# Block 0 of each later expert: its hidden rows turned by VectorE in 16 squares instead of by TensorE

## What is computed

```python
def swiglu(h, w_gate_up, w_down):
    g, u = jnp.split(h @ w_gate_up, 2, axis=-1)
    return (jax.nn.silu(g) * u) @ w_down

def moe_ffn(h, router, w_gate_up, w_down):
    ...
    for e in range(N_EXPERTS):
        out = out + combine[:, e:e + 1].astype(t.dtype) * swiglu(t, w_gate_up[e], w_down[e])
```

## Time and profile before

| what | value |
|---|---|
| median of 3 runs | 1422.05 us |
| the profiled execution's own time | 1421.34 us |
| its span | 1419.6 us |
| TensorE busy | 1412.5 us (99%) |
| VectorE busy | 1233.3 us (87%) |
| ScalarE busy | 963.5 us (68%) |
| share of TensorE in the chain that ended last | 96% |

### The profile page before, as it was taken

The page is one execution under the profiler, slowest core; times in us unless marked ns, Lnnn a source line. Parts: engine busy times, 40 slices in busy tenths (PEclk is TensorE's granted clock), DMA queues, the critical chain, the costliest instruction groups (busy, mean ns, idle before and its releaser), DMA issues.

```text
span 1419.6 us, 19929 instructions
## 1 busy us (share of the span) xinstructions
PE 1412.5 (99%) x6741; PEld 1187.1 (84%) x6741; DVE 1233.3 (87%) x1201; ACT 963.5 (68%) x839; POOL 100.2 (7%) x146
## 2 busy tenths in 40 slices
PE   9999999999999999999999999999999999999999
PEld 8998888888988888888888888888888888888887
DVE  6486888878676798899999999999998999999887
ACT  7465443443694677777777777777777777777775
POOL 3010000000022020010010000001001000000000
PEclk9999999999999999999999999999999999999999
DMA  9454655555345799999999999999999999999995
GB/s 337 146 182 145 215 201 177 177 199 166 110 176 193 260 381 393 374 373 394 387 378 394 381 367 397 391 378 384 393 366 383 394 383 373 396 384 379 384 393 196
DMA packets 212592, 442.93 MB, mean 312 GB/s; under 512 B 16372, under 2 KB 56760, under 8 KB 212544
## 3 DMA queue, kind: packets, MB, share of 16 engines
q1 hardware_dynamic: 208640, 430.18, 82.7%
q0 software_dynamic: 3888, 12.13, 2.9%
q10 hardware_dynamic: 16, 0.00, 0.0%
HBM read 434.88 MB, written 7.37 MB: 312 GB/s over the span
## 4 chain that ended last, share of the span: by engine, by line
PE 96%; DVE 2%; ACT 1%; issue 0%; POOL 0%; POOLq 0%; DVEq 0%; ACTq 0%
PE PS L1717 21%; PE PS L1716 21%; PE PS L1720 21%; PE PS L1424 5%; PE PS L1426 5%; PE PS L1425 5%; PE PS L1155 3%; PE PS L1211 2%; PE PS L1203 2%; PE PS L1205 2%; PE PS L1262 1%; PE PS L1265 1%; PE PS L1268 1%; PE PS L1185 1%; PE PS L1705 1%; PE PS L1708 1%
## 5 line engine op out<-in xcount | busy, mean ns | idle before, releaser
L1870 DVE TENSOR_TENSOR wlo<-ring,whi 128x2048 fp32r<-128x2048 f32 x334 | 758.9, 2290 | 53.7 <-ACT whi L794 51.5
L794 ACT ACTIVATE whi<-ring 128x2048 fp32r<-128x2048 f32 x334 | 639.9, 1919 | 184.5 <-PE PS L1720 171.5
L1716 PE MATMUL PS<-whi,xhi 128*128 128x512 f32 x864 | 341.1, 395 | 0.0
L1717 PE MATMUL PS<-whi,xlo 128*128 128x512 f32 x864 | 337.1, 390 | 0.0
L1720 PE MATMUL PS<-wlo,xhi 128*128 128x512 f32 x864 | 231.2, 390 | 0.0
L1720 PEld LDWEIGHTS PS<-wlo,xhi 128*128 128x128 f32 x864 | 162.2, 188 | 33.8 <-DVE wlo L1870 0.2
L1717 PEld LDWEIGHTS PS<-whi,xlo 128*128 128x128 f32 x864 | 162.6, 188 | 32.2
L1716 PEld LDWEIGHTS PS<-whi,xhi 128*128 128x128 f32 x864 | 162.3, 188 | 32.4
L1716 PE MATMUL PS<-whi,hhi 128*128 128x512 f32 x440 | 171.5, 390 | 0.0
L1717 PE MATMUL PS<-whi,hlo 128*128 128x512 f32 x440 | 171.4, 390 | 0.0
L1720 PE MATMUL PS<-wlo,hhi 128*128 128x512 f32 x440 | 117.9, 390 | 0.0
(11 more groups left out here) (381 smaller groups left out, 1638.6 us busy)
## 6 DMA issues: line engine op xcount, KB each, us to landing
ring<-in_moe_w_gate_up SPq DMA_DIRECT2D x448, 512.0 KB, 6.9
ring<-in_moe_w_down SPq DMA_DIRECT2D x224, 512.0 KB, 7.2
ring<-in_dense_w_gate_up SPq DMA_DIRECT2D x56, 512.0 KB, 4.6
ring<-in_dense_w_down SPq DMA_DIRECT2D x28, 512.0 KB, 4.1
ring<-in_a_w_in SPq DMA_DIRECT2D x12, 768.0 KB, 7.5
ring<-in_mem_w_kv SPq DMA_DIRECT2D x4, 1024.0 KB, 6.0
ring<-in_a_w_out SPq DMA_DIRECT2D x4, 1024.0 KB, 5.1
ring<-in_b_w_out SPq DMA_DIRECT2D x4, 1024.0 KB, 4.9
```

What stands on the lines that cost most here:

```text
L794: nc.scalar.activation(whi[:, j, :], ring[:, h * SLOT:(h + 1) * SLOT], ACT.Copy).then_inc(S("highs"), 1)
L1716: mm(out_, lhsT=xh, rhs=whi[:, j, c0:c0 + HD], start=begin, stop=False)
L1717: mm(out_, lhsT=xl, rhs=whi[:, j, c0:c0 + HD], start=False, stop=False)
L1870: v.tensor_tensor(wlo[:, j, :], ring[:, h * SLOT:(h + 1) * SLOT], whi[:, j, :].bitcast(F32), ALU.subtract).then_inc(S("lows"), 1)
```

## The change

In block 0 of experts 1 to 7 the four transposes on TensorE are gone; TensorE only waits for `h_ready`. VectorE turns `hnE` itself in 16 squares of 32 partitions x 128 values into an unused half of `xT` (`hnT`), eight ahead of the low part of item 1.0 and eight behind it. `hidden_high` and `hidden_low` of that turn read `hnT` in SBUF and not PSUM bank 3. Blocks 1 to 6 are as before.

```diff
+        hnT = xT[:, 0:4, CAP:2 * CAP]
...
-            def hidden_high(n):
+            def hidden_high(n, by_vector=False):
 
                 act.wait_ge(S("h_turned"), n)
-                nc.scalar.activation(hhiE, PS[:, 3, 0:4 * CAP].rearrange("p (c s) -> p c s", c=4), ACT.Copy).then_inc(S("h_high"), 1)
+                src = hnT if by_vector else PS[:, 3, 0:4 * CAP].rearrange("p (c s) -> p c s", c=4)
+                nc.scalar.activation(hhiE, src, ACT.Copy).then_inc(S("h_high"), 1)
...
-                        hidden_high(i * NBE + (NB + b))
+                        hidden_high(i * NBE + (NB + b), by_vector=b == 1 and not first)
...
-                    if b > 0 or not first:
+                    if b > 0:
                         turn_expert(i * NBE + (NB + b + 1))
+                    elif not first:
+                        pe.wait_ge(S("h_ready"), i * NBE + (NB + 1))
...
+            def turn_hidden(squares):
+
+                for n in squares:
+                    (r, c), last = divmod(n, 4), n == 15
+                    done = v.transpose(hnT[32 * c:32 * c + 32].rearrange("p k (q s) -> p k q s", q=4)[:, :, r, :],
+                                       hnE[32 * r:32 * r + 32].rearrange("p (k q f) -> p k q f", k=4, q=4)[:, :, c, :])
+                if last:
+                    done.then_inc(S("h_turned"), 1)
...
                     if b < NBE - 1:
+                        if b == 0 and not first:
+                            dve.wait_ge(S("h_ready"), i * NBE + (NB + 1))
+                            turn_hidden(range(0, 8))
                         if b > 0 or not first:
                             expert_lo(i, b + 1, 0)
+                        if b == 0 and not first:
+                            turn_hidden(range(8, 16))
                         expert_lo(i, b + 1, 1)
```

More of the change, by code:

```diff
@@ L1871, in expert_lo, with hidden_low @@
                                 ALU.subtract).then_inc(S("lows"), 1)
-            def hidden_low(n):
+            def hidden_low(n, by_vector=False):
                 dve.wait_ge(S("h_high"), n)
-                v.tensor_tensor(hloE, PS[:, 3, 0:4 * CAP].rearrange("p (c s) -> p c s", c=4), hhiE.bitcast(F32),
+                src = hnT if by_vector else PS[:, 3, 0:4 * CAP].rearrange("p (c s) -> p c s", c=4)
+                v.tensor_tensor(hloE, src, hhiE.bitcast(F32),
                                 ALU.subtract).then_inc(S("h_low"), 1)
@@ L1955, in expert @@
                         expert_lo(i, b, 2)
-                        hidden_low(i * NBE + (NB + b))
+                        hidden_low(i * NBE + (NB + b), by_vector=b == 1 and not first)
                     expert_lo(i, b, 3)
```

## The result

The changed kernel takes 1448.55 us (median of 4 runs, 1446.41 to 1451.7), the kernel before 1421.85 us (4 runs). The ratio is 1.0189, 95% interval 1.0177 to 1.0201. The direction was as forecast, the size was twice the forecast: +26.7 us against +12.7.

The account below looks back on a forecast made before the run. TensorE was taken as the bound. Low part 1.1 comes 2.27 us late, less 0.46 saved: 1.81 us in each of 7 experts, 12.7 in all; 1422.05 + 12.7 = 1434.7 us, range 1431 to 1439.

Parts of the forecast that it names:

- What bounds the kernel: TensorE, busy 99% of the span with ScalarE waiting for it: a block costs what TensorE's instructions cost, 16.78 us.
- What goes: Block 0's four transposes on TensorE: 0.46 us in each of 7 experts, 3.2 us in all.
- The squares and the two late low parts: Block 0 on VectorE: eight squares 2.52 us; low part 1.0 0.22 us late, 1.1 2.27 us late in all.
- Is more late behind it?: Later low parts, hidden rows and SP's queue: all in time, low parts 1.2 and 1.3 by 0.5 and 0.4 us.
- The rival of dearer squares: VectorE's squares cost up to 0.445 us each because of other strides, giving 1449.2 us; chance 5%.
- Long after that: Squares of the next rows, 1.78 us for four, come in block 2 at 753.73, long after the margin has grown again.
- The refill is late: Two transfers of item 2.1 land 13 us after issue: 0.8 us a time, 1440 us in all; chance 2%.
- a wait for a slot of `ring`: Sign that the prediction is wrong, if such a wait appears in the changed kernel's trace; no size given.
- The clock falls in the new wait: TensorE's wait of about 2 us halves the clock for 12 matmuls: 2.7 us an expert, 1453.7 us; chance 3%.
- The rule of the transposes: Skill's 311 ns on VectorE against 390 on TensorE would make all squares 1.24 us, a 3.2 us gain; forecast used rows.
- The crowding theory: Made after the result: late low parts delay `ring` refills, which bunch in the DMA queues and slow scatter and gather.
- The lockout: Theory made after the result: a low part on VectorE keeps GpSimd out until it ends, so scatter and gather are late.

Follow-up runs that it names:

- one square left: Changed kernel with 15 of the 16 squares left out, so block 0's hidden rows are not turned: 1419.25 us, ratio 0.9981 against the kernel before.
- the output rows first: Changed kernel, but in block 1 ScalarE scales and copies the previous expert's output rows ahead of the hidden high part: 1436.23 us, ratio 1.0098.
- the wait filled: Kernel with output rows ahead of the hidden high part, plus 12 matmuls into an unused PSUM bank before TensorE's wait for low part 1.1: 1434.94 us.
- dead squares: TensorE turns block 0's hidden rows as in the kernel before; VectorE also does the 16 squares, into a region nobody reads: 1434.73 us, ratio 1.0091.
- the token list later: Changed kernel, but in experts 1 to 6 VectorE copies the next token list in block 2, not block 1: 1435.77 us, ratio 1.0104.
- the squares at different places: Changed kernel with eight squares and output rows ahead of the hidden high part: squares behind low part 1.1, 1418.78 us; ahead of it (control), 1433.37 us.
- all squares first: Changed kernel with all 16 squares ahead of the low part of item 1.0 and none behind it: 1440.6 us, ratio 1.0132.

## Why the prediction was right in direction and wrong in size

- *What bounds the kernel*: right. Every added 1.84 us on TensorE was seen in the time.
- *What goes*: right, 0.46 us forecast, 0.47 measured with one square left.
- *The squares and the two late low parts*: right in each step. Eight squares 2.52 us; silu to silu 18.63 forecast as 18.6; 12.7 us forecast for seven experts. With the output rows first and the wait filled, or with dead squares, the whole kernel stands at 1434.9 and 1434.7 us, and the forecast was 1434.7.
- *"Is more late behind it?"* is the step that failed. It followed the late squares through the low parts, ScalarE's queue and SP's queue, but not through GpSimd's. `y_out` releases the scatter, the scatter's landing releases VectorE's copy of the next list, and the next slots release the gather. I looked at none of the three, though the copy started at 732.17 and I had its place in block 1. And I took a moved instruction to cost what it cost before, while the issue of the scatter and the small operations of GpSimd depend on what VectorE does beside them. The runs put 13.8 us on it (the changed kernel less the one with dead squares). The rival of dearer squares had 1449.2 us, close to the 1448.55 measured; that is chance, the squares cost what the row said.
- *"Long after that"*, said of the squares of the next rows, failed for the same reason: they waited up to 2.8 us for the gather.
- *The refill is late*, a rival: a wait for a slot of `ring` was named as a sign of being wrong, and it did appear, 11.9 us in 17 waits of ScalarE in experts 1 to 7. But VectorE's delay of the refills is the same with dead squares, where nothing but the direct term is lost; and with the token list later ScalarE waits for slots even longer, 30.8 us in 39 waits, and experts 1 to 6 lose only the direct term. It does not decide here.
- *The clock falls in the new wait*, a rival at 3%: it was there, but in two of seven experts of the profiled run, and a fall costs 1.6 us where I had 2.7. In the changed kernel a fall cost nothing on balance: the expert with it loses 1.6 us more in block 1 and less in the blocks behind, since VectorE catches up meanwhile. Where nothing else is late it costs 1.3 us a run (1436.23 against 1434.94).
- *The rule of the transposes* (the Trainium skill, "VectorE: DVE Perf Modes", The three transpose paths: 311 ns against 390 ns): the trace decides for the row, 0.303 us for each square of 32 partitions.

The crowding theory fell with the output rows first and with the dead squares: refills as late as in the changed kernel, and a scatter that landed in 6.1 to 6.6 us. The two kernels with the squares at different places alone do not settle it, since moving the squares also moves refills. The lockout holds for the small operation. In the twelve profiles 98 of GpSimd's small operations in experts 1 to 7 start under an instruction of VectorE with two inputs in SBUF, and every one ends 0.05 us after the end of such an instruction. The Trainium skill ("SBUF — State Buffer", Summary: rules for kernel authors) states that where VectorE has two inputs in SBUF and GpSimd's operation reads SBUF, the second to start fully blocks until the first finishes. The traces agree, with those 0.05 us. The squares have one input.

The issue of the scatter waits in the same way. In the same profiles 49 scatters are issued under such an instruction, and each issue ends 1.47 to 1.53 us after the end of it; the other 35 issues take 1.60 to 1.66 us. The kernel with one square shows it best: its issue starts under the low part of the hidden rows, which reads `xT` and `hhi` in SBUF and is short.

```profile
723.63 0.69 DVE L1881 TENSOR_TENSOR hlo<-xT,hhi 128x512 fp32r<-128x512 f32 x1
```

```profile
723.91 1.88 POOL L694 DMA_INDIRECT acc<-xn,arena  x1 [0.16 <-issue]
```

That low part ends at 724.32, the issue at 725.79. In the kernel before, the same low part has one input in PSUM, and the issue under it takes 1.61 us. Three things stay open: what the issue needs at its start, why the scatter takes longer to land also after a slow issue has ended, and why the small operation sometimes gets in between two low parts that run back to back (0.62 us) and sometimes waits out both (4.36 us).

No version here beats the kernel before with the whole work done. Free squares would bring 3.3 us at most. Eight squares behind the low part of item 1.1, with the output rows first, are free, but half a turn only; the 16 need 5.05 us where, by the forecast's walk, VectorE has room for 2.78 ahead of the low part of item 1.1. Squares spread over later items, where VectorE gains on TensorE again, were not tried.

## What to carry to other kernels

When work is moved onto an engine with little idle time, its idle time is the first thing to lose: ask who else lives in it. Here GpSimd, once it started under one of VectorE's two-input instructions, got on only when such an instruction ended, and the same eight squares at two places made kernels 14.6 us apart. Follow a delay through every queue that it releases, up to the wait that comes back to the engine you started from, and look for waits in the trace of before that ended just in time: they have no margin.

## What was not expected of the hardware

- A GpSimd operation on one element takes 0.18 us when VectorE is idle or does squares, and up to 4.37 us when VectorE runs two low parts back to back. It can wait out both.
- The issue of an indirect scatter on GpSimd takes 1.60 to 1.66 us, 3.47 to 3.53 under a low part of 128x2048, and 1.87 to 1.93 under one of 128x512 with both inputs in SBUF: it depends on what VectorE does when it starts.
- A wait of TensorE of up to 2.3 us (2.8 with all squares first) brought the granted clock to its lower level in 1 to 3 of seven experts in four profiles, and in none in two: with the token list later (2.3 us) and with dead squares (1.9 us). With 12 matmuls in that wait there was no fall in the profile.
